# Norms behind the two down projections of a two-block transformer kernel: squares shared by GpSimd and TensorE, an early weight item, low halves last

## What is computed

```
sh1, sc1, g1, sh2, sc2, g2 = split(silu(c) @ ada_w[i] + ada_b[i], 6)      # modulation
y = rms_norm(h, g) = h * rsqrt(mean(h*h) + EPS) * g
h = h + g1 * mixer(rms_norm(h) * (1 + sc1) + sh1)
h = h + g2 * ffn(rms_norm(h) * (1 + sc2) + sh2)
ffn(a) = (silu(conv(a @ w_up)[:, :F]) * conv(a @ w_up)[:, F:]) @ w_down
```

## Time and profile before

| what | value |
|---|---|
| median of three executions | 1953.19 us |
| the profiled execution, its own time | 1952.28 us |
| its span in the trace | 1950.5 us |
| TensorE busy | 1834.0 us, 94% of the span |
| VectorE busy | 746.0 us, 38% |
| ScalarE busy | 614.8 us, 32% |
| GpSimd busy | 89.5 us, 5% |
| DMA, share of 16 engines | 74% |
| mean granted TensorE clock | 0.98 |

### The profile page before, as it was taken

The page is one execution under the profiler, slowest core; times in us unless marked ns, Lnnn a source line. Parts: engine busy times, 40 slices in busy tenths (PEclk is TensorE's granted clock), DMA queues, the critical chain, the costliest instruction groups (busy, mean ns, idle before and its releaser), DMA issues.

```text
span 1950.5 us, 29825 instructions
## 1 busy us (share of the span) xinstructions
PE 1834.0 (94%) x12110; PEld 1256.9 (64%) x12110; DVE 746.0 (38%) x1575; ACT 614.8 (32%) x1093; POOL 89.5 (5%) x108
## 2 busy tenths in 40 slices
PE   5999999989999998999999999999999999999997
PEld 4855899979899998968444444444444444444446
DVE  2575677546577644275221121121221221221216
ACT  3465555434455535365111111111111110110115
POOL 0010211010111101001000000000000000000001
PEclk8999999989999998989899999999999999999998
DMA  9638545454555553203999999999999999999991
GB/s 395 253 159 340 218 183 176 171 208 181 190 221 182 187 181 140 107 2 150 374 427 425 424 427 424 426 428 425 426 428 425 426 428 425 427 426 426 428 423 49
DMA packets 64942, 592.81 MB, mean 304 GB/s; under 512 B 6000, under 2 KB 9328, under 8 KB 10448
## 3 DMA queue, kind: packets, MB, share of 16 engines
q1 hardware_dynamic: 64416, 589.75, 74.1%
q10 hardware_dynamic: 432, 1.71, 0.2%
HBM read 590.39 MB, written 1.05 MB: 303 GB/s over the span
## 4 chain that ended last, share of the span: by engine, by line
PE 51%; DMA 28%; DVE 10%; ACT 7%; issue 2%; POOL 1%; SPq 1%; ACTq 0%; DVEq 0%; POOLq 0%
DMA ring<-in_experts 27%; PE ps L2349 15%; DVE wd_lo L1173 6%; ACT wd_hi L715 5%; PE ps L2359 3%; PE ps L1854 3%; PE ps L1850 3%; PE ps L1851 3%; PE ps L2336 2%; PE ps L1903 2%; PE ps L2118 2%; PE ps L2113 2%; PE ps L2114 2%; PE ps L1868 1%; PE ps L1869 1%
## 5 line engine op out<-in xcount | busy, mean ns | idle before, releaser
L2349 PE MATMUL ps<-ring,A 128*64 128x512 f32 x2112 | 468.3, 597 | 39.1 <-ACT A L1055 22.7
L2349 PEld LDWEIGHTS ps<-ring,A 128*64 128x64 f32 x2112 | 168.8, 137 | 333.9 <-issue 333.0
L1713 DVE TENSOR_TENSOR A<-ps,W 128x512 f32<-128x512 f32 x66 | 45.4, 688 | 788.9 <-PE ps L2386 788.9
L1173 DVE TENSOR_TENSOR wd_lo<-ring,wd_hi 128x2048 fp32r<-128x2048 f32 x107 | 245.7, 2299 | 187.8 <-ACT wd_hi L715 187.8
L1850 PE MATMUL ps<-aL_hi,wd_hi 128*128 128x256 f32 x1040 | 256.8, 285 | 3.7 <-ACT wd_hi L715 2.0
L1851 PE MATMUL ps<-aL_lo,wd_hi 128*128 128x256 f32 x1040 | 254.9, 283 | 0.0
L715 ACT ACTIVATE wd_hi<-ring 128x2048 fp32r<-128x2048 f32 x107 | 203.7, 1905 | 120.4 <-PE ps L2118 67.5
L2359 PE MATMUL ps<-ring,A 128*64 128x512 f32 x1056 | 233.9, 596 | 0.0
L1850 PEld LDWEIGHTS ps<-aL_hi,wd_hi 128*128 128x128 f32 x1040 | 199.4, 192 | 6.5 <-issue 5.3
L1851 PEld LDWEIGHTS ps<-aL_lo,wd_hi 128*128 128x128 f32 x1040 | 199.9, 192 | 0.1
L1044 ACT ACTIVATE A<-ps 128x512 f32<-128x512 f32 x66 | 39.4, 597 | 472.7 <-PE ps L2349 472.7
(11 more groups left out here) (362 smaller groups left out, 2225.2 us busy)
## 6 DMA issues: line engine op xcount, KB each, us to landing
ring<-in_experts SPq DMA_DIRECT2D x198, 2048.0 KB, 17.2
ring<-in_weights SPq DMA_DIRECT2D x161, 1024.0 KB, 4.9
hT<-in_x SPq DMA_DIRECT2D x1, 1024.0 KB, 7.4
hT<-in_ctx SPq DMA_DIRECT2D x1, 1024.0 KB, 15.0
hT<-in_weights SPq DMA_DIRECT2D x1, 1024.0 KB, 5.8
tab<-in_tables ACTq DMA_DIRECT2D x1, 768.0 KB, 10.3
out<-aT SPq DMA_DIRECT2D x2, 384.0 KB, 2.6
A<-in_tables SPq DMA_DIRECT2D x1, 548.0 KB, 6.0
```

The lines of the kernel that those rows point to most:

```text
L1173: dve.tensor_tensor(wd_lo[:, b], cell(PLAN[name]["first"][k]["cell"]), wd_hi[:, b].bitcast(F32), ALU.subtract).then_inc(split_lo, 1)
L1713: dve.tensor_tensor(m_gl[:, j].rearrange("p c h n -> p (c h) n"), ps[:, 6 + j, :].rearrange("p (c n) -> p c n", c=8), b_up[:, bass.ds(e * ...
L2349: mm = pe.matmul(ps[h * CAP:(h + 1) * CAP, 4 + j, :], xg[:, c, :], w[:, c, h], start=(c == 0), stop=(c == KC - 1))
```

## The change

It has five parts.

1. `RUNS`: item 0 of `sc_in` is loaded between `down0` and the modulation items 40 to 43, in the cell that was left out there; item 1 and the others follow behind them. All items up to `up1` 1 are given cells anew. Thereby ada items 44 to 47 take the cells of `sc_in` 11, `sc_out` 0, 1 and 2 (before: `sc_in` 10 and 11, `sc_out` 0 and 1), `up1` 0 that of `sc_out` 3 (before `sc_out` 2) and `up1` 1 that of `sc_in` 10 (before `sc_out` 3). `sc_in` 2 to 6 take the cells of `sc_in` 0 and of ada 40 to 43 (before: of ada 40 to 43 and of `sc_in` 0).
2. Norms 2 and 4: GpSimd adds squares 0 to 4 only, in four additions; squares 5, 6 and 7 go to TensorE one by one, beside the sum of the others. Norms 1 and 3 keep six additions.
3. Norm 2: TensorE computes all sums first and the whole group of modulation weights behind them. The wait for seven updated chunks goes.
4. Behind both down products VectorE updates all eight chunks and computes the low half of the next stage's item 0 behind them.
5. `split_tokens` does the eight chunks with the high weights first, for each of its outputs, then waits for the low half and does the eight with the low weights.

```diff
-RUNS = [..., ("up0", 0, 22), ("down0", 0, 11), ("ada", 40, 4), ("sc_in", 0, 12), ("sc_out", 0, 4), ("ada", 44, 4), ("up1", 0, 22), ...]
+RUNS = [..., ("up0", 0, 22), ("down0", 0, 11), ("sc_in", 0, 1), ("ada", 40, 4), ("sc_in", 1, 11), ("sc_out", 0, 4), ("ada", 44, 4), ("up1", 0, 22), ...]
...
+        ADDED_CHUNKS = {1: KC - 1, 2: 5, 3: KC - 1, 4: 5}
         def added(n):
-            return (n - 1) * (KC - 2)
+            return sum(ADDED_CHUNKS[m] - 1 for m in range(1, n))
...
             def norm_squares(n):
-                for c in range(1, KC - 1):
+                for c in range(1, ADDED_CHUNKS[n]):
...
-                residual(ffn_sem["down"], T, 48 * L + 40, {4: (after, 0)}, KC * L)
+                residual(ffn_sem["down"], T, 48 * L + 40, {}, KC * L)
+                split_item(after, 0)
...
                 pe.wait_ge(split_hi, split_count(name, k))
-                pe.wait_ge(split_lo, split_count(name, k))
                 for s, out in enumerate(outs):
+                    tokens = slice((first + s) * P, (first + s + 1) * P)
                     for c in range(KC):
-                        tokens = slice((first + s) * P, (first + s + 1) * P)
                         pe.matmul(out, a_hi[:, c, tokens], wd_hi[:, b, c, :], start=(c == 0), stop=False)
-                        pe.matmul(out, a_hi[:, c, tokens], wd_lo[:, b, c, :], start=False, stop=False)
-                        mm = pe.matmul(out, a_lo[:, c, tokens], wd_hi[:, b, c, :], start=False, stop=(c == KC - 1))
+                        pe.matmul(out, a_lo[:, c, tokens], wd_hi[:, b, c, :], start=False, stop=False)
+                    pe.wait_ge(split_lo, split_count(name, k))
+                    for c in range(KC):
+                        mm = pe.matmul(out, a_hi[:, c, tokens], wd_lo[:, b, c, :], start=False, stop=(c == KC - 1))
...
             def norm(n):
+                bank, last = NORMS[n]["bank"], ADDED_CHUNKS[n]
+                def chunk(c):
+                    pe.wait_ge(norm_sq, 8 * n + c + 1)
+                    pe.matmul(ps[:, bank, 0:T], table("mean"), sq4[:, c % 3, :], start=(c == last), stop=(c == KC - 1)).then_inc(norm_sum, 1)
                 def sums():
-                    bank = NORMS[n]["bank"]
-                    pe.wait_ge(x_acc, added(n) + KC - 2)
-                    pe.matmul(ps[:, bank, 0:T], table("mean"), sq4[:, 3, :], start=True, stop=False).then_inc(norm_sum, 1)
+                    for c in range(last, KC - 1):
+                        chunk(c)
+                    pe.wait_ge(x_acc, added(n + 1))
+                    pe.matmul(ps[:, bank, 0:T], table("mean"), sq4[:, 3, :], start=(last == KC - 1), stop=False).then_inc(norm_sum, last)
                     pe.wait_ge(norm_sq, 8 * n + KC)
-                    pe.matmul(..., sq4[:, (KC - 1) % 3, :], start=False, stop=True).then_inc(norm_sum, 7)
-                if n in NORM_GROUPS:
-                    pe.wait_ge(h_updated, NORMS[n]["ready"] - 1)
-                    ada(NORM_GROUPS[n], sums)
+                    pe.matmul(..., sq4[:, (KC - 1) % 3, :], start=False, stop=True).then_inc(norm_sum, 1)
+                if n != 2:
+                    if n in NORM_GROUPS:
+                        pe.wait_ge(h_updated, NORMS[n]["ready"] - 1)
+                        ada(NORM_GROUPS[n], sums)
+                    else:
+                        sums()
                 else:
                     sums()
+                    ada(NORM_GROUPS[n])
```

More of the change, by code:

```diff
@@ L98 @@
 RUNS = [("ada", 0, 8), ("qkv", 2, 2), ("ada", 8, 4), ("qkv", 4, 2), ("qkv", 0, 2), ("ada", 12, 24), ("win_out", 0, 4), ("ada", 36, 4), ("up0", 0, 22),
-        ("down0", 0, 11), ("ada", 40, 4), ("sc_in", 0, 12), ("sc_out", 0, 4), ("ada", 44, 4), ("up1", 0, 22), ("down1", 0, 11),
+        ("down0", 0, 11), ("sc_in", 0, 1), ("ada", 40, 4), ("sc_in", 1, 11), ("sc_out", 0, 4), ("ada", 44, 4), ("up1", 0, 22), ("down1", 0, 11),
         ("w_in", 0, 11), ("cmp", 0, 2), ("w_out", 0, 4), ("moe", 0, CELLS), ("gate", 0, 4)]
@@ L1929, in norm @@
             def norm(n):
+                bank, last = NORMS[n]["bank"], ADDED_CHUNKS[n]
+                def chunk(c):
+                    pe.wait_ge(norm_sq, 8 * n + c + 1)
+                    pe.matmul(ps[:, bank, 0:T], table("mean"), sq4[:, c % 3, :], start=(c == last), stop=(c == KC - 1)).then_inc(norm_sum, 1)
                 def sums():
-                    bank = NORMS[n]["bank"]
-                    pe.wait_ge(x_acc, added(n) + KC - 2)
-                    pe.matmul(ps[:, bank, 0:T], table("mean"), sq4[:, 3, :], start=True, stop=False).then_inc(norm_sum, 1)
+                    for c in range(last, KC - 1):
+                        chunk(c)
+                    pe.wait_ge(x_acc, added(n + 1))
+                    pe.matmul(ps[:, bank, 0:T], table("mean"), sq4[:, 3, :], start=(last == KC - 1), stop=False).then_inc(norm_sum, last)
                     pe.wait_ge(norm_sq, 8 * n + KC)
-                    pe.matmul(ps[:, bank, 0:T], table("mean"), sq4[:, (KC - 1) % 3, :], start=False, stop=True).then_inc(norm_sum, 7)
-                if n in NORM_GROUPS:
-                    pe.wait_ge(h_updated, NORMS[n]["ready"] - 1)
-                    ada(NORM_GROUPS[n], sums)
+                    pe.matmul(ps[:, bank, 0:T], table("mean"), sq4[:, (KC - 1) % 3, :], start=False, stop=True).then_inc(norm_sum, 1)
+                if n != 2:
[4 more added lines that the diff above has]
+                        sums()
                 else:
                     sums()
+                    ada(NORM_GROUPS[n])
             def window_qkv():
```

## The result

The changed kernel took 1940.63 us (median of six executions, 1937.95 to 1943.08); the kernel before, on the same chip in between, took 1952.58 (six, 1950.93 to 1953.66). The ratio is 0.9941, interval 0.9931 to 0.995. Run again later the changed kernel took 1942.95 (five; ratio 0.9956, interval 0.9942 to 0.9969). Its eleven executions have a median of 1941.92. The forecast was 1942.2, with a range of 1938.0 to 1947.5. As a difference to the kernel before, 11.0 us were forecast; the first set measured 11.95, the second 8.4. The profiled execution after is the longest of its six, 1943.08. The two profiled executions are 9.2 us apart.

A forecast was written before the change was run, and what follows sets the result against it. The prediction took waits at the norms, where TensorE stands still, as the bound. Gains 7.1 + 3.5 + 1.9 less loss 1.5 make 11.0: profiled 1952.28 becomes 1941.3, the median 0.9 higher, 1942.2 us, range 1938.0 to 1947.5.

The forecast's parts named there:

- Norm 2: Between the last down instruction and the next product: first tile at 421.0 instead of 428.11, gain 7.1 us.
- 0.73 for an addition beside updates: GpSimd's additions beside running updates were taken at 0.73 us each, from a possible 0.73 to 2.6.
- the bound of 0.7: In norms 2 and 4, a late last addition could delay VectorE's low half, making the sum up to 0.7 us a norm worse.
- Norm 4: Same plan as norm 2 without a late item: reciprocal at 732.5 instead of 736.00, gain 3.5 us.
- Norm 3: `up1` 0 lands later, delaying rounding, low half and sixth addition; sums end at 530.65 instead of 529.15, loss 1.5 us.
- Low weights last: At item 2 of `w_in`, 16 instructions go ahead of the wait for the low half: gain 1.9 us, bounds 0 and 2.4.
- a microsecond gained at a norm comes out at the end: The expert stage starts when the first block is done, so time gained or lost at a norm should reach the end.
- A: Rival: norm 3 loses the clock through pauses of 1.5 and 1.3, costing up to 5 us: 1947.2; chance 0.10.
- B: Rival: TensorE loses the clock during norm 2's sums, gain 4.4 instead of 7.1: 1946.9; chance 0.07.
- C: Rival: only the early item counts, additions beside updates taking 2.6 us each in norms 2 and 4: 1952.8; chance 0.04.
- D: Rival: slower than before, `up1` 0 landing late at norm 3, loss 15.3 against gains of 12.5: 1956.0; chance 0.03.
- E: Rival: gain not all passed on around attention and the first expert, plus or minus 3 us; forecast with this spread 0.74.

The follow-up runs named there:

- e7: The changed kernel with the order of loads (`RUNS`) of the kernel before, so without the early `sc_in` 0: 1943.63 us.
- e4: The changed kernel with `up1` 0 loaded ahead of modulation items 44 to 47: 1940.56 us, ratio 0.9943.
- e5: The kernel before with only part 5, low weights last in token products: 1952.15 us, ratio 1.0001.
- e6: The kernel before with only part 1, the new order of loads (`RUNS`): 1949.35 us, ratio 0.9986.
- e2: The changed kernel with six additions by GpSimd in norms 2 and 4 as before: 1951.59 us, ratio 0.9999.
- e1: The changed kernel run again with no edit: 1942.95 us.
- e9: The changed kernel with the 32 gate products split, one half ahead of item 9 of `w_in`: 1938.79 us, ratio 0.9937.
- e10: The changed kernel with `up1` 0 loaded ahead of modulation items 44 to 47 and the gate products split: 1940.04 us, ratio 0.9942.
- e8: The changed kernel with TensorE's order in norm 2 as before, eight modulation instructions ahead of the sums: 1940.24 us.

## Why the prediction was right, point by point

**Norm 2, 7.1 forecast, 7.14 measured.** With 0.6 taken off, the trace has: rounding 409.3 (forecast 409), additions done 415.3 (415.4), square 7 done 415.9 (415.9), sums done 416.8 (416.9), root done 417.3 (417.4), low half 415.4 to 417.7 (the same), reciprocal 417.6 (417.6), modulation group done 420.4 (420.6), first tile 421.0 (421.0). The choice that carried this was 0.73 for an addition beside updates. The prediction called that pace unseen, but norm 4 of before has it: the first and third additions lie beside updates and took 0.74 and 0.73. In all fourteen traces an addition that started inside a low half took 2.1 to 2.8 us, every other one at most 0.75 (one a trace, which started in the last 0.1 us of a low half, among the latter). The Trainium skill (SBUF — State Buffer, Who interferes with whom) says that a VectorE instruction with two inputs in SBUF contends with a GpSimd instruction that reads SBUF, and that one with at most one, outside the two-port modes, does not. The low half has two, an update takes one from PSUM; with that rule the traces agree. In e7 the low half began 0.3 us into an addition and took 2.58 instead of 2.28, and the addition behind it 2583 ns, which is how the prediction had read that page: a late addition delays VectorE as well. The row that the prediction weighed against it, the low half at 727.38, couldn't tell: only 0.12 us of the addition beside it was left. In the changed kernel the last one ended 0.1 us ahead of the low half, so the bound of 0.7 wasn't reached.

**Norm 4, 3.5 forecast, 3.56 measured.** That the clock would fall as before was wrong in size. It fell at 731.7, but for 3.4 us instead of 10.2:

```profile
731.70:735.10 3.40, 3.40 (x18) 3.40 (x17) 3.40 (x10) 1.98 (x5) 0.00 (x0) 0.50 0.01 2
```

That gave 0.8 more: from the reciprocal to `w_in` 2 it is 16.65 us where it was 19.89, and 2.4 of the difference is TensorE's earlier start there (it waits 0.15 us and not 2.57). The prediction counted TensorE's idle time at the end of the norm (4.0) and left out the wait for GpSimd ahead of the sums, 3.96 in the trace of before, which went away.

**Norm 3, loss 1.5 forecast, 1.65 measured.** Rounding, low half and the blocked addition came in the order described; ScalarE's rounding came 2.5 later against chunk 0's update, 2.4 forecast. e4 shows the cell to be the cause.

**Low weights last, 1.9 forecast, 2.0 measured at the place**, and 0.25 by the time the experts start (e5). The pause between high and low was 0.15 us in e5 and in the changed kernel, where half a microsecond was forecast. The step that failed is not a term but the sentence that a microsecond gained at a norm comes out at the end. For norms 2 and 4 it holds. It doesn't hold at the compression: 11.0 was forecast, 11.8 was gained by its first product and 10.1 was left of it at the end. The two misses, 0.8 of clock at norm 4 and 1.7 at the compression, partly cancel; the total is close for that reason as well, and that part is luck.

**Rivals.** A, norm 3 losing the clock: its pauses in the changed kernel were 1.6 and 1.3, and it stayed at 2.4 GHz in every profile. B: norm 2 kept the clock in the changed kernel; e7 shows the same norm at 1.2 GHz when the pause grows to 4.16, sums and the start of the group included, so the mechanism is real and its condition wasn't met. C, only the early item: e6 gives what it is worth alone, 2.3 us. Its mechanism, additions slow beside updates, shows in no trace. Its outcome, no gain from parts 2 and 4, is e2's, where a low half blocks the fifth addition. D, `up1` 0 landing late: the three transfers issued from 507.7 to 513.8 landed in 4.7 to 6.9 us. E, not all passed on: this is what happened, within its 3 us. The Trainium skill (TensorE: Matmul & The Clock Gate, What's actually happening) has the chip judge activity in a free-running window. By it the same pauses can fall either way. Norm 4, the same to 0.01 us in the changed kernel and e4, had 3.4 us at 1.2 GHz behind it in one and 6.8 in the other; with that rule the traces agree.

**What stays open.** The start of the experts takes about 209 or about 207 us. The six traces with the long one all have 3.4 us at 1.2 GHz right behind the last root and 13.7 later, the eight with the short one have 10.2 or 13.7 in all. Why wasn't tried; both occur with the same kernel (after and e1). Nor was the part ahead of norm 2, which varies at least as much. How much of the spread of the executions each makes isn't shown, since only one execution of a set has a trace. What it is about the gate products that goes with the fall was tested by splitting them only.

**Best version.** e9 has the lowest median, 1938.79, and e10, e8 and e4 follow within 1.8; their intervals overlap. Against e1 of the changed kernel it is 4.2 faster and against its first set 1.8, but e9 and e1 ran on different chips, and the ratio of the first set (0.9931 to 0.995) lies within e9's (0.9924 to 0.995) while e1's (0.9942 to 0.9969) overlaps it. So 1.7 us for the split is seen in the traces' compression and not shown in the time. e10 has the shortest norms.

## What to carry to other kernels

An addition on GpSimd and a long VectorE operation with both inputs in SBUF don't mix: count both queues and see that one has run out before the other starts. Shortening GpSimd's part and moving VectorE's long operation are one step: in norm 4 they gave 2.15 and nothing alone and 3.55 together.

When items of a ring are dealt anew, look at the item behind the next boundary as well: the early item was worth 3.85 at its norm and cost 1.6 at the next one, which one further entry in the order of loads gave back at that norm.

A gain should be followed in the trace past its place, to the next point where the engine's clock changes. Where a total doesn't show an edit's gain, compare the stages: most repeat to 0.2 us, while sets of the same kernel differed by 2.3 us in their medians.

## What was unexpected of the hardware

TensorE's clock fell to 1.2 GHz behind 5.00 of 5.00 us in which the engine was busy, the last 3.75 with the 32 narrow gate products. It stayed there for 3.4 us, busy throughout, and cost 1.7 us. In the six traces with this fall TensorE had no gap in the 12 us ahead of the first compression product: here no idle time was needed for a fall.

A blocked addition ends 0.6 us behind the low half that blocks it, whenever it started: in norm 3 the low half ended at 522.48, the addition at 523.07, and all 85 blocked additions of the fourteen traces ended 0.58 to 0.60 behind. It looks held until the low half is done rather than slowed: it takes 2.1 to 2.8 us, where 0.73 is usual, by how early in the low half it starts.
